# Delta rule masks: five groups' clipped differences on another engine, exponentials a chunk sooner, one wait exchanged

## The reference, cut to what matters

```
g = cumsum(g); diff = g[..., :, None] - g[..., None, :]
decay = where(incl, exp(where(incl, diff, 0.0)), 0.0)
a_mat = where(strict, einsum('bhnid,bhnjd->bhnij', kb, k) * decay, 0.0)
qk = where(incl, einsum('bhnid,bhnjd->bhnij', q, k) * decay, 0.0)
```

## Time and profile before

| | |
|---|---|
| median of 3 runs | 888.3 us (887.1 to 889.78) |
| the profiled execution | 889.81 us, of which its span 887.9 us |
| PE busy | 858.1 us (97%) |
| DVE busy | 722.1 us (81%) |
| ACT busy | 499.5 us (56%) |
| the chain that ended last | PE 73%, DVE 16%, ACT 7% |
| PE's granted clock, mean | 0.996 |

### The profile page before, as it was taken

How to read it: one execution, slowest core, us unless ns; L and a number is a source line. 1 busy time by engine, 2 the same in 40 slices (tenths; PEclk the granted TensorE clock), 3 DMA queues, 4 the chain that set the end, 5 groups by cost and what they waited for, 6 DMA issues and landing times.

```text
span 887.9 us, 15315 instructions
## 1 busy us (share of the span) xinstructions
PE 858.1 (97%) x5840; PEld 770.4 (87%) x5840; DVE 722.1 (81%) x1140; ACT 499.5 (56%) x743; POOL 46.7 (5%) x48
## 2 busy tenths in 40 slices
PE   6999899999899999999999989999999999999997
PEld 6999798888777888888888789999887789999996
DVE  6686989845766888888879778999999999946774
ACT  7789756656356555555555564333346675445742
POOL 0001210221010000000000000000001220001000
PEclk9999899999999999999999999999999999999999
DMA  8763774610483477777796636455454536564441
GB/s 260 241 238 85 234 228 144 182 52 1 168 278 123 158 252 255 258 258 260 260 325 203 224 102 208 157 178 187 153 189 143 178 99 223 174 200 159 143 143 48
DMA packets 139664, 163.65 MB, mean 184 GB/s; under 512 B 17203, under 2 KB 112347, under 8 KB 139483
## 3 DMA queue, kind: packets, MB, share of 16 engines
q1 hardware_dynamic: 139611, 162.92, 56.1%
HBM read 158.68 MB, written 4.23 MB: 183 GB/s over the span
## 4 chain that ended last, share of the span: by engine, by line
PE 73%; DVE 16%; ACT 7%; issue 2%; DMA 2%; SPq 0%; DVEq 0%; ACTq 0%
PE psum L504 15%; PE psum L506 15%; PE psum L505 15%; PE psum L545 14%; PE psum L546 7%; DVE w_lo L1436 4%; DVE cv L1916 3%; PE psum L800 2%; ACT w_hi L970 2%; DVE Tq L1676 1%; DVE outer L1674 1%; DVE cacc L1596 1%; DMA w_raw<-in_gdn_w_out_dram 1%; ACT PT L1101 1%; PE psum L907 1%
## 5 line engine op out<-in xcount | busy, mean ns | idle before, releaser
L1436 DVE TENSOR_TENSOR w_lo<-w_raw,w_hi 128x1024 fp32r<-128x1024 f32 x264 | 316.4, 1223 | 85.8 <-ACT w_hi L970 83.7
L970 ACT ACTIVATE w_hi<-w_raw 128x1024 fp32r<-128x1024 f32 x264 | 275.4, 1057 | 192.2 <-PE psum L506 148.9
L504 PE MATMUL psum<-hT,w_hi 128*128 128x256 f32 x704 | 203.0, 288 | 3.8 <-DVE w_lo L1436 1.9
L505 PE MATMUL psum<-hT,w_hi 128*128 128x256 f32 x704 | 200.1, 284 | 0.0
L506 PE MATMUL psum<-hT,w_lo 128*128 128x256 f32 x704 | 200.0, 284 | 0.0
L545 PE MATMUL psum<-hT,w_hi 128*128 128x512 f32 x512 | 181.0, 399 | 0.6 <-DVE hT L1509 0.6
L546 PE MATMUL psum<-hT,w_lo 128*128 128x256 f32 x512 | 143.8, 281 | 0.0
L504 PEld LDWEIGHTS psum<-hT,w_hi 128*128 128x128 f32 x704 | 136.1, 193 | 6.1 <-issue 3.3
L505 PEld LDWEIGHTS psum<-hT,w_hi 128*128 128x128 f32 x704 | 136.0, 193 | 0.4 <-issue 0.2
L506 PEld LDWEIGHTS psum<-hT,w_lo 128*128 128x128 f32 x704 | 136.0, 193 | 0.0
L545 PEld LDWEIGHTS psum<-hT,w_hi 128*128 128x128 f32 x512 | 96.2, 188 | 25.1 <-issue 1.2
(11 more groups left out here) (297 smaller groups left out, 1196.7 us busy)
## 6 DMA issues: line engine op xcount, KB each, us to landing
w_raw<-in_w_in_dram SPq DMA_DIRECT2D x44, 1024.0 KB, 5.0
w_raw<-in_sc_w_in_dram SPq DMA_DIRECT2D x32, 1024.0 KB, 7.4
w_raw<-in_gdn_w_in_dram SPq DMA_DIRECT2D x23, 1024.0 KB, 6.7
ada<-in_w_ada_dram SPq DMA_DIRECT2D x24, 512.0 KB, 5.2
w_raw<-in_gdn_w_out_dram SPq DMA_DIRECT2D x8, 1024.0 KB, 5.4
w_raw<-in_sc_w_out_dram SPq DMA_DIRECT2D x8, 1024.0 KB, 8.0
w_raw<-in_w_ret_out_dram SPq DMA_DIRECT2D x8, 1024.0 KB, 5.1
w_raw<-in_w_conv_out_dram SPq DMA_DIRECT2D x4, 1024.0 KB, 5.7
```

Source lines behind the costliest of these rows:

```text
L504: pe.matmul(o, l_hi, r_hi, start=start, stop=False, skip_group_check=True)
L505: pe.matmul(o, l_hi, r_lo, start=False, stop=False, skip_group_check=True)
L970: act.activation(w_hi[j % 2 * 2 + h][:, :, :], raw[slot][:, h * KH2:(h + 1) * KH2, :], ACT.Copy).then_inc(hi_ready, 1)
L1436: return dve.tensor_tensor(o, whole, hi.bitcast(F32), ALU.subtract)
```

## The change

Four tables and their users change:

- The clipped differences of the groups 0, 1, 2 (turn 7) and 4, 5 (turn 8) are made by DVE with a two-operation instruction, min(G - bias, 0), four a group. In turn 7 they stand between the splits of (8,1) and (9,0), in turn 8 between those of (9,1) and (10,0). ACT keeps group 3, now in turn 7, and the groups 6 and 7 in turn 10. The exponential of a DVE group is taken with scale 1.0 in place of -1.0.
- The exponentials of the groups 4 to 7 are taken in turn 11 in place of 12. The products (`MASKS`) and key products (`KEYS`) keep their turns.
- Key product 7 waits for `nbT_ready` alone, no longer for `pt_ready` at 5.
- The semaphore `ang_ready` gives way to a count on `ang_step`, so that the number of semaphores stays the same.

```
-FALLS = {7: (0, 1, 2), 8: (3,), 9: (4, 5), 10: (6, 7)}
-EXPS = {8: (0, 1, 2, 3), 12: (4, 5, 6, 7)}
+FALLS = {7: (3,), 10: (6, 7)}
+FALLS_V = {7: (0, 1, 2), 8: (4, 5)}
+FALLS_ORDER = (0, 1, 2, 4, 5)
+EXPS = {8: (0, 1, 2, 3), 11: (4, 5, 6, 7)}
 MASKS = {8: (0, 1), 9: (2,), 10: (3,), 12: (4, 5), 13: (6, 7)}
+ANGLE_STEPS = 12
...
                 pe.wait_ge(qkv_ready, 5 + p)
-                if n >= 3:
+                if 3 <= n < 7:
                     pe.wait_ge(pt_ready, n - 2)
                 elif n == 0:
                     pe.wait_ge(lnss_ready, 1)
-                if n == 7:
+                elif n == 7:
                     pe.wait_ge(nbT_ready, 1)
...
-                act.wait_ge(fall_ready, n + 1)
+                if n in FALLS_ORDER:
+                    act.wait_ge(fall_v_ready, FALLS_ORDER.index(n) + 1)
+                else:
+                    act.wait_ge(fall_ready, (3, 6, 7).index(n) + 1)
...
+            def falls(n):
+                p, c = n // NT, n % NT
+                dve.wait_ge(grow_loaded, 16)
+                for a in range(HG):
+                    g = G_ROW + HG * p + a
+                    i = dve.tensor_scalar(PT[:, c, HG * p + a, :], G[:, HG * p + a, c * P:(c + 1) * P], bgt[:, c, g:g + 1], 0.0, ALU.subtract, ALU.min)
+                i.then_inc(fall_v_ready, 1)
...
                 split_lo(0, 0, c + 1, 1)
+                for n in FALLS_V.get(c, ()):
+                    falls(n)
                 split_lo(0, 0, c + 2, 0)
...
-                    act.wait_ge(ang_ready, 1)
+                    act.wait_ge(ang_step, ANGLE_STEPS)
```

More of the change, by code:

```diff
@@ L283, in build @@
         mod_done, mod_ready, gain2_ready = sem("mod_done"), sem("mod_ready"), sem("gain2_ready")
-        glu_ready, ang_step, ang_ready, trig_ready = (
-            sem(n) for n in ("glu_ready", "ang_step", "ang_ready", "trig_ready"))
+        glu_ready, ang_step, fall_v_ready, trig_ready = (
+            sem(n) for n in ("glu_ready", "ang_step", "fall_v_ready", "trig_ready"))
         rp_step = sem("rp_step")
@@ L1097, in exps @@
                 p, c = n // NT, n % NT
-                act.wait_ge(fall_ready, n + 1)
+                if n in FALLS_ORDER:
+                    act.wait_ge(fall_v_ready, FALLS_ORDER.index(n) + 1)
+                else:
+                    act.wait_ge(fall_ready, (3, 6, 7).index(n) + 1)
                 for e in range(2):
                     two = PT[:, c, HG * p + 2 * e:HG * p + 2 * e + 2, :]
-                    i = act.activation(two, two, ACT.Exp, scale=-1.0, bias=lnr[:, c, 2 * p + e:2 * p + e + 1])
+                    i = act.activation(two, two, ACT.Exp, scale=1.0 if n in FALLS_ORDER else -1.0, bias=lnr[:, c, 2 * p + e:2 * p + e + 1])
                 i.then_inc(e_ready, 1)
@@ L1890, in angles @@
                 angle(dve.tensor_tensor(cos_t, cos_t, ang[:, :], ALU.add))
-                dve.tensor_scalar(cos_t, cos_t, lim, -lim, ALU.min, ALU.max).then_inc(ang_ready, 1)
+                dve.tensor_scalar(cos_t, cos_t, lim, -lim, ALU.min, ALU.max).then_inc(ang_step, 1)
+                assert angle_steps[0] + 1 == ANGLE_STEPS
             halves = y_norm(1, "sc_out", between=shift_scale_gate)
```

## The result

The changed kernel takes 883.5 us (median; 880.2 to 886.4) beside 889.7 (887.1 to 891.3) for the kernel before, measured together. The ratio is 0.9927, with a 95% interval from 0.991 to 0.9944: 6.2 us by the medians. The forecast was 881.3 for a start of 888.3, 7.0 us. The changed kernel's profiled execution took 883.9 us, of which its span was 881.9.

A forecast was written before the change was run, and what follows sets the result against it. PE, busy 97% of the span, bounds the kernel, so only its idle or slow time can go. PE gains 8.1 us, but DVE's later solve limits this to 7.0: 888.3 to 881.3 us, range 879.8 to 884.8.

The forecast's parts named there:

- Rival (d): Key product 7's wait is for the silu, or scratch trips hold the solve: only 1.85 us gained, 886.5; chance 0.06.
- Part 1: ACT, turns 7 and 8: five groups leave, ACT is 1.9 us earlier at w_hi(10,0); w_lo(10,0) moves from 78.45 to 76.6.
- Part 2: DVE, turns 7 and 8: the five groups cost 0.21 us an instruction, 2.5 and 1.7 us, covered by idle time.
- Rival (c): DVE's groups cost as much as hx, 0.54 us each: 4.7 of the 7.0 us go, 886.0; chance 0.04.
- Parts 3 and 4: PE to chunk 12 comes 1.85 us earlier; at key product 7, 4.1 us idle and 2.4 low-clock loss go: 8.1 at z.
- Part 5: Exponentials in ACT's turn 11, w_hi(13,1) over at 101.0; DVE then needs 24.0 us, solve gains 6.7, taken as 7.0.
- rival (b): ACT late in turn 11, each table load holding it 1.4 us longer: DVE 2.8 later, 884.1; chance 0.07.
- The rest: Solve's block loads come some 5 us earlier, slack remains; both engines shift alike afterwards, so 7.0 us reach the end.
- Rival (a): PE's clock falls at the wait for Tc, grown from 0.4 to 1.5 us: 2.4 us or more lost, 884; chance 0.09.
- (e): Slower: low clock after the Tc wait persists through the rounds of small products, adding 21.6 us, 903; chance 0.03.

The follow-up runs named there:

- e1: Kernel before with one edit: key product 7 waits for nbT_ready alone; 886.9 us for 888.8, ratio 0.998.
- e5: Changed kernel with each of the 20 DVE clipped differences made twice; one execution only, solve 1.61 us later than the changed kernel's.
- e3: Kernel before with only the five groups' clipped differences moved to DVE, old wait and old turn of the exponentials; ratio 0.9971 to the kernel before.
- e6: Kernel before plus eleven idle matmuls ahead of key product 7, so PE waits busy; ratio 0.9963 to the kernel before.
- third comparison: The unaltered changed kernel timed a third time beside the kernel before: 884.9 us for 890.7, ratio 0.9946.
- e7: Changed kernel with the small DVE steps nb and nbeg of turn 9 put ahead of the products; ratio 0.989, again 0.9934, to the kernel before.
- e8: e7 plus three idle matmuls ahead of PE's wait for Tc; 883.2 us for e7's 884.2, ratio 0.9925 to the kernel before.
- e9: e1 plus four idle matmuls ahead of PE's wait for Tc; 886.3 us for 890.7 of the kernel before, ratio 0.9953.
- e4: Changed kernel with one part undone: key product 7 waits for the fifth pt_ready again; ratio 0.9954 to the kernel before.
- e2: Kernel before with key product 7 waiting for nbT_ready alone and exponentials of groups 4 to 7 in turn 11; ratio 0.9956.

## Why the prediction was right

**What PE waited for.** Right: the wait was for `pt_ready`, not for the silu named as its releaser. e1 takes it away with ACT's order unchanged. Rival (d) falls.

**Part 1, ACT's relief.** w_lo(10,0) comes 15.93 us after the first key product for 17.68, 1.75 sooner; 1.85 was forecast.

**Part 2, DVE's price.** The estimate from `gdiag` holds: 12 take 2.44 us and 8 take 1.65, 0.20 each for the 0.21 taken, and both lie in idle time. Rival (c) falls, and e5 shows what it would have cost by the same mechanism.

**Parts 3 and 4, PE.** The forecast was 8.1 us at z; it is 8.22. Of this 1.77 is the shift that e3 shows alone, 4.14 the idle time, and 2.3 the clock, which e6 measures by itself. Key product 7 was put near 102 and starts at 102.45 in a trace that began 0.57 later.

**Part 5, DVE as the later one.** By hand 6.7 came out for the solve, 7.3 with the closer gaps; 7.0 was taken and 6.71 is measured (why, below). The wait for `Tc`, put at 1.5, is 1.52. ACT in turn 11 did as the rows said: the load back to back with the exponentials, and w_hi(13,1) before 102 (ACT's timeline of the changed kernel):

```profile
92.44 1.28 ACT L1107 ACT_TABLE_LOAD   x1
93.74 3.30 ACT L1107 ACTIVATE PT<-PT,lnr 128x256 f32<-128x256 f32 x8
...
100.71 1.99 ACT L973 ACTIVATE w_hi<-w_raw 128x1024 fp32r<-128x1024 f32 x2
```

The first exponential starts 1.30 us after the load. The drain of 1.38 us more that the Trainium skill, page "ScalarE: Activation LUTs", section "What ACT_TABLE_LOAD costs", counts into a switch is not there, and rival (b) falls with it. w_hi(13,1), the first of the last row, is over at 101.77, where 101.0 was forecast; 0.57 of the difference is the later start of this trace. DVE takes it at once:

```profile
101.79 2.36 DVE L1442 TENSOR_TENSOR w_lo<-w_raw,w_hi 128x1024 fp32r<-128x1024 f32 x2 [0.20 <-ACT w_hi L973]
```

From there to the solve it needs 23.73 us, forecast 24.0. So the closer gaps did bring 0.27 of the 0.3 that was added for them, and w_hi(13,1), 0.2 later than forecast, took most of it back. That the figure by hand came out exactly is two small errors that cancel.

**The rest.** The slack of the block loads was mis-sized, which cost nothing here. It was put at 5 us; it is 2.4. SP's queue in the profile after:

```profile
111.15 0.49 SPq L351 DMA_DIRECT2D w_raw<-in_gdn_w_in_dram  x1
112.02 1.68 SPq L410 DMA_DIRECT2D l_scratch<-LT  x2
120.17 0.85 SPq L415 DMA_DIRECT2D Lq<-l_scratch  x2
```

The last blocks' writes are issued from 112.02, 5.0 us sooner than before (117.05), but 0.9 us behind a load of 1 MB of weights, where 4.4 us had lain between the two. They land only near 120, and the read back is issued at 120.17 for 120.92 in the earlier trace rows: of 5.0 us on the way in, 0.75 are left (5.6 and 1.3, counted from the first key product). It landed at 123.1, and the solve began at 125.52. If everything else came 2.4 us sooner still and this trip stayed where it is, it would be the bound of the solve.

**From the solve to the end.** All of it comes through in the trace to `Tc`, 7.10 us. That both engines are shifted alike from there on holds until the output projection. There the profile before has a wait of PE for `w_lo` of 1.63 us, at 240.5, whose weights landed late (ACT waits 0.97 us for them); the changed kernel's three profiles have 0.6, and their gain is 8.0 to 8.2 us from then on. The prediction had nothing of this, and with one profile of the kernel before nothing shows whether its wait comes every time. The time shows 5.9 to 7.2, less than the traces. The median of the first comparison, 883.5, lies 2.2 above the forecast; of these 0.8 is the smaller gain, and the rest is the kernel before measured at 889.7 where the forecast started from 888.3. In the third comparison the changed kernel's median, 884.9, even lies 0.1 above the upper bound of the forecast, 884.8, with its kernel before at 890.7: the gain was foreseen better than the time.

**Rivals (a) and (e).** The mechanism of (a) is real, and e1's profile shows it: a wait of 1.87 us there was followed by 3.4 us at the low level. In the changed kernel's profiles the wait was 1.5 to 1.7 and the clock stayed at 1.00. The mean clocks of the timed executions say that it doesn't always. In all the profiles the last 0.4 to 3.5 us of the span are at the low level, which alone brings the mean to 0.998 at the lowest. Of the 26 executions of the changed kernel four have 0.997 and three 0.996, which takes over 6 us of low clock; of the 25 of e7, e8 and e9 none is below 0.998. In the first comparison the four lower ones have a median of 884.8 us, the other eight 882.3. So the clock does fall somewhere else in some executions and takes back part of the gain; that it is at `Tc` is likely, since e7 waits less there and the others wait busy, but no trace of the changed kernel shows it. Rival (a), with a chance of 0.09, was nearer than the profiles let it seem. (e) falls with e1 too: behind the fallen clock the small products did bring it back, within 3.4 us.

## What to carry to other kernels

Where a view names a releaser, ask the code which semaphore value the instruction waits for, and look which instruction ended just before under that name: here two ended within 0.1 us of each other, and the one not named was the one that mattered. When a wait is taken away, price the low clock behind it separately, and work out which engine is second: here the exchanged wait alone brought 3.9 us at the solve, and with the second engine relieved as well 6.7. Before work is moved onto another engine's idle time, size that idle time: 4.1 us were free, 2.2 more would have been, and after that each us costs one.

## What the runs showed of the hardware

**A DVE product of two SBUF tensors is held by GpSimd.** `nbeg`, 32 columns, takes 1.21 us beside GpSimd's multiply and 0.19 alone. In the changed kernel the two end together, 87.26 + 1.21 = 88.47 and 87.14 + 1.28 = 88.42, and they did so in the kernel before, at 89.66 and 89.61 (its timelines of DVE and GpSimd):

```profile
88.45 1.21 DVE L1662 TENSOR_TENSOR nbeg<-nb,eg 128x32 f32<-128x32 f32 x1
...
88.32 1.29 POOL L1391 TENSOR_TENSOR PT<-PT,keep 128x512 f32<-128x512 f32 x1 [4.63 <-DVE PT L1615]
```

The Trainium skill, page "GPSIMD Engine Reference", section "8. Key points", says that GpSimd shares its SBUF interfaces with VectorE and contends with instructions that have two SBUF inputs. The trace agrees, and gives the size: the DVE instruction is held until the whole multiply is done. It is not the only one: in the trace of the kernel before, a later step (L1916, `cv<-aP,par,cv`) takes 0.48 us in the median of 240, and 1.52 where it starts 0.2 us behind a GpSimd product of 1.45 (L1418, at 680.06), ending 0.28 after it.

**The clock falls for waits shorter than the one that was in question, and not each time.** PE's idle times of 4.0, 4.0 and 3.0 us were followed by the lower level for 6.8, 3.4 and 3.4 us (before, e3, e4), one of 1.87 by 3.4 us (e1), waits of 1.0 to 1.7 (changed, e2, e5, e7) in seven profiles by none. One of e1's twelve timed executions has a mean clock of 1.000, so it didn't fall there either. Matmuls whose result nobody reads kept it at 1.00 through two of these waits.

**Small writes behind a large load.** Two writes of 256 KB issued 0.9 and 2.2 us behind a load of 1 MB landed 6.0 and 6.8 us after their issue; in the profile before the same two, 4.4 and 5.7 us behind it, took 2.7 and 2.5.
